# Expert weights in 32 KB runs: halves of 4 MB in the loop, smaller pieces and a new order of work for the last two experts

## The chip, the cores and the metric

One core of a Trainium2 chip. The metric is device time in microseconds (us) of one launch, lower is better; a time is the median of several runs.

## What is computed

One decoder layer for 256 prompt tokens with 16 meta tokens ahead of them, and 8 sample tokens: two mixers, then a mixture of 32 experts with 4 of them for each token, then a last norm. All weights are fp32, and nearly all the bytes are the experts': `w_gu` is 32 x 1024 x 2048 (8 MB an expert), `w_down` 32 x 1024 x 1024 (4 MB an expert), 403 MB of the 431 MB read.

```python
x = x + (g_a * branch_a + g_b * branch_b) @ w_o
logits = (xt @ w_router) + b_router                  # xt = rms_norm(x, g_ffn)
gates = softmax(top_k(logits, 4))
# for each expert e, over the tokens that chose it:
hgu = xblk @ w_gu[e] + b_gu[e]
gate = minimum(hgu[:, :1024], 7.0)
up = clip(hgu[:, 1024:], -7.0, 7.0)
act = gate * sigmoid(1.702 * gate) * (up + 1)
y = act @ w_down[e] + b_down[e]                      # times the gate, added to x by token
y_prompt, y_sample = rms_norm(x, g_final)            # meta tokens dropped
```

## The kernel before

**Front, up to about 175 us.** The input projection, both mixers and `w_o` run in split precision. Then, tile by tile (two of 128 tokens, one of the 8 samples), the new rows `Y` are normed, turned and routed. For the gather, a row of `Y` times its norm is kept as three bf16 parts in `XP`: ScalarE's `part` (L732) rounds the first, VectorE's `keep_rest` (L1477) subtracts it, `next_part` and `keep_third` make the other two. The first expert has a shorter way (L1101).

**An expert is an item i** (64 token slots; `more` further rounds exist for fuller experts and are not run here). TensorE does, in this order: `gate_up(i)`, eight rows k of `gu_ring`, each 4 products of 128 x 512 (shown as x8); the scatter of expert i-2 after rows 2, 4 and 6 (one token tile each, high and low parts into banks 6 and 7); `way_back(i-1)`, which turns `pick_twice` into the matrix that sends slots back to tokens; `gather` for i+1; `down(i-1)`, eight rows of `down_ring`; `turn(i)`, which transposes gate and up. Around it ScalarE copies the gate half (`keep_gate`), takes the sigmoid, copies the way back (`back`) and rounds the expert's result to `y_high` (`high`); VectorE does the SwiGLU (`swiglu`), adds scattered rows to `Y` (`add_rows`, L1628), makes `pick_twice` (`make_twice`, L1592 to L1596) and `pick`, copies the up half and makes `y_low` (`low_part`).

**Loads.** All of the experts' weights come by SyncE (SP), one queue, in program order. `gu_ring` has 16 slots of one row (8 KB a partition), eight for even and eight for odd experts; `down_ring` has eight slots of 4 KB. `load_gu` (L419 to L423) brings two rows in one load of 2 MB: partition p takes matrix rows 2p and 2p+1 of a block of 256, so a run is 16 KB. `load_row` brings one row, 1 MB in runs of 8 KB. `load_down` brings four rows, 2 MB in runs of 16 KB. Each load waits until TensorE has used what lay in its slots: `gu_used` counts rows of gate-up, `down_used` pairs of rows of down. The order is gate-up of i+2, then down of i, with the second half of a gate-up put behind the down for experts 9 to 19 (`HALVED`). The last expert's down weights go to slots 0 to 3 of `gu_ring` in four loads of 1 MB (L542), once gate-up of expert 30 is done.

**Deal of the rows.** Since row k of a gate-up block holds matrix rows of one residue, every operand of that product follows it: the transposes of `Y` (`by_row`), the gather's slices of `XP`, `wr`, `g_ffn`.

**The end.** For the last two: `gate_up(31)`, `way_back(30)`, `turn(31)`, `down(30)`, `way_back(31, 5)`, then `down(31)` with the scatters of 30 after its rows 1, 3 and 5 into banks 6, 0 and 2 (`LAST_BANKS`), then the scatters of 31, the additions, the norm (L593, L1717, L1719) and the stores.

## Time and profile before

| | |
|---|---|
| median of 3 runs | 1090.71 us (1090.71 to 1091.31) |
| the profiled execution | 1091.32 us, its span 1089.5 us |
| TensorE (PE) busy | 1049.2 us, 96% |
| VectorE, ScalarE busy | 462.5 us, 174.2 us |
| read from HBM | 431.10 MB, 397 GB/s over the span |

A busy PE is a PE with matmuls in it, also while they are fed slowly. How much of the span each stage takes and what it waits for must be read from the slices, the chain of work and the timeline. In a timeline row the bracket names how long the engine was idle before and what ended that; PEld are the weight loads of TensorE, SPq is SyncE's queue, in which only the issue of a load shows, not its transfer.

### The profile page before, as it was taken

Reading aid. Unit: us, or ns where it says so; the run is one execution under the profiler, and the core shown is the slowest. Engines: PE = TensorE matmul, PEld = TensorE weight load, DVE = VectorE, ACT = ScalarE, POOL = GpSimd, SP = SyncE. Lnnn points to the kernel's source line nnn. Section 1 sums busy time; section 2 is a strip of 40 time slices with the busy share of each in tenths; the row PEclk is TensorE's granted clock in tenths of the full one; section 3 lists DMA queues with packets and bytes.
Section 4 is the critical chain, followed back from the end, with each engine's and each line's share of the span. In section 5 each row is a group of like instructions: output and inputs, shape, how many; then the busy total and the mean of one; then the engine's idle time right before and its main releaser. Section 6 shows DMA issues by size and latency. Waiting matters only on the chain.

```text
span 1089.5 us, 17315 instructions
## 1 busy us (share of the span) xinstructions
PE 1049.2 (96%) x7081; PEld 510.2 (47%) x7081; DVE 462.5 (42%) x780; ACT 174.2 (16%) x296; POOL 8.9 (1%) x21
## 2 busy tenths in 40 slices
PE   8999999999999999999999999999999999999995
PEld 7999975434433444434344333333444333333332
DVE  5577675333333333333333333333333333333344
ACT  5435533100000000000000000000000000000012
POOL 1000100000000000000000000000000000000000
PEclk9999999999999999999999999999999999999998
DMA  9872899999999999999999999999999999999994
GB/s 295 289 227 103 324 405 375 429 420 426 428 429 427 429 428 430 427 429 428 429 428 428 429 428 428 428 429 428 428 429 428 429 428 429 429 428 431 426 425 170
DMA packets 52479, 432.63 MB, mean 397 GB/s; under 512 B 4630, under 2 KB 21546, under 8 KB 26205
## 3 DMA queue, kind: packets, MB, share of 16 engines
q1 hardware_dynamic: 50959, 431.04, 95.3%
q10 hardware_dynamic: 1494, 1.22, 0.4%
q8 instruction: 19, 0.31, 0.1%
q14 instruction: 7, 0.06, 0.0%
HBM read 431.10 MB, written 1.39 MB: 397 GB/s over the span
## 4 chain that ended last, share of the span: by engine, by line
PE 65%; DMA 26%; DVE 4%; issue 4%; ACT 1%; SPq 1%; DVEq 0%; ACTq 0%
PE PS L1153 24%; PE PS L1182 17%; DMA down_ring<-in_w_down_dram 14%; DMA gu_ring<-in_w_gu_dram 11%; PE PS L918 9%; PE PS L1082 3%; PE PS L1122 2%; PE PS L949 2%; PE PS L1124 1%; PE PS L1196 1%; PE PS L1166 1%; PE PS L1164 1%; DVE pick_twice L1596 1%; PE PS L1200 1%; PE PS L869 0%
## 5 line engine op out<-in xcount | busy, mean ns | idle before, releaser
L1153 PE MATMUL PS<-gu_ring,XgT 128*64 128x512 f32 x2048 | 470.5, 599 | 6.7 <-DMA gu_ring<-in_w_gu_dram 6.7
L1153 PEld LDWEIGHTS PS<-gu_ring,XgT 128*64 128x64 f32 x2048 | 134.5, 136 | 272.0 <-issue 244.5
L1182 PE MATMUL PS<-down_ring,actT 128*64 128x512 f32 x984 | 219.3, 596 | 7.7 <-DMA down_ring<-in_w_down_dram 7.7
L1628 DVE TENSOR_TENSOR Y<-PS,Y 128x1024 f32<-128x1024 f32 (+1 forms) x96 | 117.0, 1220 | 253.7 <-PE PS L1124 253.7
L1182 PEld LDWEIGHTS PS<-down_ring,actT 128*64 128x64 f32 x984 | 67.5, 137 | 134.8 <-issue 119.3
L1666 DVE SCALAR_TENSOR_TENSOR y_low<-PS,slot_gate,y_high 128x512 fp32r<-128x512 f32 x31 | 23.3, 750 | 228.6 <-ACT y_high L804 228.6
L816 ACT ACTIVATE work<-PS 128x512 f32<-128x512 f32 x32 | 19.1, 597 | 454.8 <-PE PS L1153 454.8
L918 PE MATMUL PS<-h_high,win_high 128*128 128x264 f32 (+2 forms) x256 | 71.2, 287 | 0.0
L918 PE MATMUL PS<-h_high,win_low 128*128 128x264 f32 (+2 forms) x256 | 70.9, 286 | 0.0
L918 PE MATMUL PS<-h_low,win_high 128*128 128x264 f32 (+2 forms) x256 | 70.8, 285 | 0.0
L804 ACT ACTIVATE y_high<-PS,slot_gate 128x512 fp32r<-128x512 f32 x31 | 21.3, 687 | 258.9 <-PE PS L1182 258.9
L1082 PE MATMUL PS<-pick,XP 128*128 128x64 bf16 x1768 | 56.7, 193 | 0.0
L1082 PEld LDWEIGHTS PS<-pick,XP 128*128 128x128 bf16 x1768 | 56.1, 99 | 0.8 <-issue 0.8
L1122 PEld LDWEIGHTS PS<-y_high,spread 64*128 64x128 f32 x186 | 17.3, 183 | 75.5 <-issue 74.6
L918 PEld LDWEIGHTS PS<-h_high,win_high 128*128 128x128 f32 x256 | 47.4, 189 | 0.4 <-issue 0.2
L1317 DVE TENSOR_TENSOR win_low<-gu_ring,win_high 128x2048 fp32r<-128x2048 f32 x15 | 34.4, 2293 | 30.7 <-ACT win_high L619 30.6
L918 PEld LDWEIGHTS PS<-h_low,win_high 128*128 128x128 f32 x256 | 47.4, 188 | 0.0
L918 PEld LDWEIGHTS PS<-h_high,win_low 128*128 128x128 f32 x256 | 47.3, 188 | 0.0
L1122 PE MATMUL PS<-y_high,spread 64*128 64x512 f32 x186 | 46.6, 498 | 0.0
L1643 DVE TENSOR_TENSOR work<-PS,bias_gu 128x512 f32<-128x512 f32 x64 | 44.0, 687 | 1.2 <-PE PS L1200 0.6
L1564 DVE TENSOR_TENSOR XgT<-PS,params 128x512 f32<-128x512 f32 x31 | 21.4, 691 | 53.5 <-PE PS L1082 53.5
L1124 PE MATMUL PS<-y_low,spread 64*128 64x512 f32 x186 | 36.6, 391 | 0.0
(236 smaller groups left out, 778.2 us busy)
## 6 DMA issues: line engine op xcount, KB each, us to landing
gu_ring<-in_w_gu_dram SPq DMA_DIRECT2D x119, 2048.0 KB, 28.5
down_ring<-in_w_down_dram SPq DMA_DIRECT2D x60, 2048.0 KB, 21.2
gu_ring<-in_w_gu_dram SPq DMA_DIRECT2D x18, 1024.0 KB, 10.0
gu_ring<-in_w_in_dram SPq DMA_DIRECT2D x16, 1024.0 KB, 9.4
gu_ring<-in_w_down_dram SPq DMA_DIRECT2D x4, 1024.0 KB, 28.3
down_ring<-in_w_down_dram SPq DMA_DIRECT2D x3, 1024.0 KB, 9.4
down_ring<-in_w_pool_up_dram SPq DMA_DIRECT2D x1, 2048.0 KB, 11.6
gu_ring<-in_w_conv_out_dram SPq DMA_DIRECT2D x2, 1024.0 KB, 6.2
```

Of the source, the lines that this page charges most:

```text
L918: return mm(PS[:, n % 4, 0:COLS - lo], w[:, k, P * (n % 2):P * (n % 2) + P], h[:, k, lo:COLS], start=first, stop=final)
L949: last = mm(PS[:, 4 + n % 4, 0:TOK], of(w, k, m), x[:, k, :], start=(k == 0 and part == 0), stop=(k == CH - 1 and part == 2))
L1082: last = mm(rows if rows is not None else PS[:, 5, SLOTS * k:SLOTS * k + SLOTS], XP[:, part, 2 * P * m:2 * P * m + 2 * P].rearrange("t (p ...
L1122: mm(PS[:, bank + h, :], way[rows, t, :], y_high[rows, :], start=True, stop=False)
L1124: last = mm(PS[:, bank + h, :], way[rows, t, :], y_low[rows, :], start=False, stop=True)
L1153: last = mm(PS[SLOTS * h:SLOTS * h + SLOTS, b, :], XgT[:, k, :], w[:, D * b + HALF * h:D * b + HALF * h + HALF], start=(k == 0), stop=(k = ...
L1182: last = mm(PS[SLOTS * h:SLOTS * h + SLOTS, bank, :], acts[:, f % 4, f // 4, :], rows[:, f, HALF * h:HALF * h + HALF], start=(f == 0), sto ...
L1317: tt(win_low[:, b % WIN_SLOTS, :], gu_ring[:, b % WIN_SLOTS, :], win_high[:, b % 2, :].bitcast(F32), ALU.subtract).then_inc(win_ready, 1)
L1564: tt(XgT[:], PS[:, 5, :].rearrange("p (k s) -> p k s", k=KT), g_ffn_cols.unsqueeze(2).to_broadcast([P, KT, SLOTS]), ALU.mult).then_inc(xg_ ...
L1628: tt(Y[rows, t, :].rearrange("p (h n) -> p h n", h=2), PS[rows, bank:bank + 2, :], Y[rows, t, :].rearrange("p (h n) -> p h n", h=2), ALU.a ...
L1643: tt(hgu[:, HALF * b:HALF * b + HALF].rearrange("p (c s) -> p c s", s=SLOTS), PS[:, 2 + b, :].rearrange("p (c s) -> p c s", s=SLOTS), bias ...
L1666: stt(y_low[:], PS[:, bank, :], gate[:], y_high[:].bitcast(F32), ALU.mult, ALU.subtract).then_inc(low_ready, 1)
```

## The change

Gate-up weights come in loads of 4 MB (`load_half`): partition p takes four matrix rows of a block of 512, a run of 32 KB. One semaphore for each half (`half_landed`) takes the place of one for each two rows, and TensorE waits at rows 0 and 4. The loads of expert 2 and the first half of expert 3 stay in smaller pieces, with semaphores of their own. The deal of rows goes from two to four everywhere: `by_row`, `wr`, `g_ffn`; `part` and `keep_rest` now read `Y` in steps of four elements (`dealt`) and write `XP` in row order, so that the gather reads it without a step. Three single bf16 products (`fill_early`) are added in the front.

At the end, expert 30 comes in 2 MB pieces, expert 31's rows 0 to 3 in two of 2 MB and 4 to 7 in four of 1 MB, the down weights of 30 in four of 1 MB, those of 31 in three of 1 MB and two of 512 KB. Both last ways back move into the last gate-up, behind rows 3 and 5, with `spread_last` now for expert 30 and `spread` for 31; `turn(31)` moves behind two rows of `down(30)`. The last scatters are split: all high parts first, then the low parts. On VectorE `make_twice` moves ahead of the row additions, in every item. The diff, cut to what the text speaks of (the rest are `wr`, `g_ffn`, the new semaphores, and calls that follow):

```diff
--- before.py
+++ after.py
...
@@ -218,6 +218,12 @@
         pool_up = down_ring[:, CH:2 * CH, :]
         pool_high = by_rows(win_low[:, 4:6, :])
         conv_out, conv_low, conv_high = gu_ring[:, 0:2, :], win_low[:, 0:2, :], win_low[:, 2:4, :]
+
+        def dealt(cols):
+            return cols.rearrange("t (p r) -> t r p", r=CH)
+
+        def by_fours(cols):
+            return cols.rearrange("t (r p) -> t r p", r=CH)
...
@@ -412,16 +425,23 @@
...
-            def load_row(e, parity, k):
-                m, r = divmod(k, 2)
+            def load_row(e, parity, k, signal=None):
+                h, r = divmod(k, CH)
                 sp.dma_start(gu_ring[:, KT * parity + k, :],
-                             w_gu[0, e, 2 * P * m:2 * P * m + 2 * P, :].rearrange("(p r) n -> p r n", r=2)[:, r, :]
-                             ).then_inc(gu_landed[CH * parity + m], 16)
-
-            def load_gu(e, parity, m):
-                src = w_gu[0, bass.ds(e, 1), 2 * P * m:2 * P * m + 2 * P, :].rearrange("a (p r) n -> (a p) (r n)", r=2)
+                             w_gu[0, e, HALF * h:HALF * h + HALF, :].rearrange("(p r) n -> p r n", r=CH)[:, r, :]
+                             ).then_inc(signal or gu_landed[CH * parity + k // 2], 16)
+
+            def load_gu(e, parity, m, signal):
+                h, q = divmod(m, 2)
+                src = w_gu[0, bass.ds(e, 1), HALF * h:HALF * h + HALF, :].rearrange("a (p q r) n -> (a p) q (r n)", q=2, r=2)
                 sp.dma_start(gu_ring[:, KT * parity + 2 * m:KT * parity + 2 * m + 2, :].rearrange("p s n -> p (s n)"),
-                             src).then_inc(gu_landed[CH * parity + m], 16)
+                             src[:, q, :]).then_inc(signal, 16)
+
+            def load_half(e, parity, h):
+                src = w_gu[0, bass.ds(e, 1), HALF * h:HALF * h + HALF, :].rearrange("a (p r) n -> (a p) (r n)", r=CH)
+                at = KT * parity + CH * h
+                sp.dma_start(gu_ring[:, at:at + CH, :].rearrange("p s n -> p (s n)"), src
+                             ).then_inc(half_landed[2 * parity + h], 16)
...
@@ -467,17 +487,24 @@
...
-            def item_gu(i, e, parity, chunks=range(CH)):
-                for m in chunks:
-                    sp.wait_ge(gu_used, 8 * i + (2 * m - 14))
-                    load_gu(e, parity, m)
+            def item_gu(i, e, parity, halves=range(2)):
+                for h in halves:
+                    sp.wait_ge(gu_used, 8 * i + (4 * h - 12))
+                    load_half(e, parity, h)
+
+            def item_chunk(i, e, parity, m, signal):
+                sp.wait_ge(gu_used, 8 * i + (2 * m - 14))
+                load_gu(e, parity, m, signal)
 
 
             for k in range(2):
                 sp.wait_ge(gu_used, k + 1)
-                load_row(2, 0, k)
-            item_gu(2, 2, 0, (1, 2, 3))
-            item_gu(3, 3, 1)
+                load_row(2, 0, k, third_rows)
+            for m, signal in ((1, half_landed[0]), (2, third_chunk), (3, half_landed[1])):
+                item_chunk(2, 2, 0, m, signal)
+            for m, signal in ((0, fourth_chunk), (1, half_landed[2])):
+                item_chunk(3, 3, 1, m, signal)
+            item_gu(3, 3, 1, (1,))
...
@@ -493,7 +520,7 @@
...
-            first, second = (0, 1), (2, 3)
+            first, second = (0,), (1,)
...
@@ -512,7 +539,7 @@
...
-            with sp.Fori(0, E // 2 - 2 - AHEAD - HALVED) as pair:
+            with sp.Fori(0, E // 2 - 3 - AHEAD - HALVED) as pair:
...
@@ -527,22 +554,37 @@
...
+            before, last = more * E + (E - 2), more * E + (E - 1)
+            for m in range(CH):
+                item_chunk(before, E - 2, 0, m, gu_landed[m])
+            item_down(more * E + (E - 3), E - 3)
+            for m in range(2):
+                item_chunk(last, E - 1, 1, m, gu_landed[CH + m])
+            for k in range(CH, KT):
+                sp.wait_ge(gu_used, 8 * last + (k - 15))
+                load_row(E - 1, 1, k, last_rows[k - CH])
+
+            def down_rows(e, first, n):
+                h, j = divmod(first, CH)
+                return w_down[0, e, HALF * h:HALF * h + HALF, :].rearrange("(p j) n -> p j n", j=CH)[:, j:j + n, :]
+
+            for q in range(CH):
+                sp.wait_ge(down_used, 4 * before + (q - 3))
+                sp.dma_start(down_ring[:, 2 * q:2 * q + 2, :], down_rows(E - 2, 2 * q, 2)).then_inc(before_landed[q], 16)
             sp.wait_ge(gu_used, more * (8 * E) + 8 * (E - 1))
-            for q in range(CH):
-                h, j = q // 2, 2 * (q % 2)
-                sp.dma_start(down_last[:, 2 * q:2 * q + 2, :],
-                             w_down[0, E - 1, HALF * h:HALF * h + HALF, :].rearrange("(p j) n -> p j n", j=CH
-                                                                                     )[:, j:j + 2, :]
-                             ).then_inc(last_landed[q], 16)
+            for q in range(CH - 1):
+                sp.dma_start(down_last[:, 2 * q:2 * q + 2, :], down_rows(E - 1, 2 * q, 2)).then_inc(last_landed[q], 16)
+            sp.dma_start(down_last[:, 6:7, :], down_rows(E - 1, 6, 1)).then_inc(last_landed[3], 16)
+            sp.dma_start(down_last[:, 7:8, :], down_rows(E - 1, 7, 1)).then_inc(last_row_landed, 16)
...
@@ -729,7 +771,7 @@
...
-                nc.scalar.activation(dst, Y[rows, t, cols], ACT.Copy, scale=stat[rows, 3, t:t + 1]
+                nc.scalar.activation(by_fours(dst), dealt(Y[rows, t, cols]), ACT.Copy, scale=stat[rows, 3, t:t + 1]
                                      ).then_inc(first_part, 1)
...
@@ -844,13 +886,18 @@
...
             last, before = more * E + (E - 1), more * E + (E - 2)
-            keep_gate(last, False, before)
+            sigmoid(before)
+            back(before, spread_last, slot_gate_last)
+            act.wait_ge(scattered, more * (3 * E) + 3 * (E - 2))
+            back(last, spread, slot_gate, 5)
+            act.wait_ge(gu_used, more * (8 * E) + 8 * E)
+            act.wait_ge(act_ready, before + 1)
+            nc.scalar.activation(hgu[:, 0:HALF], PS[:, 0, :], ACT.Copy).then_inc(gate_kept, 1)
             sigmoid(last)
             nc.scalar.preload_act_table(ACT.Sqrt)
-            back(last, spread_last, slot_gate_last, 5)
-            high(before)
+            high(before, slot_gate_last)
             act.wait_ge(scattered, more * (3 * E) + 3 * (E - 1))
-            high(last, slot_gate_last, 5)
+            high(last, slot_gate, 5)
...
@@ -1020,6 +1067,10 @@
...
+
+            def fill_early():
+                mm(PS[:, 1, :].rearrange("p (c n) -> p c n", c=CH), ones[:], ones[:].unsqueeze(1).to_broadcast([P, CH, P]),
+                   start=True, stop=True)
...
@@ -1067,9 +1118,11 @@
...
             pe.wait_ge(pick_early, 1)
+            fill_early()
             pe.wait_ge(resid, 5)
             turn_rows(1, 1)
             turn_tails()
+            fill_early()
             pe.wait_ge(x2_kept, 5)
...
@@ -1088,6 +1140,7 @@
...
+            fill_early()
             pe.wait_ge(mask_ready, 3)
             count(1, ones[:], 2, True, False)
...
@@ -1116,12 +1169,19 @@
...
-            def scatter(t, way=spread, bank=6):
+            def scatter_part(t, way, part, first):
+
+                for h in range(2):
+                    rows = slice(SLOTS * h, SLOTS * h + SLOTS)
+                    last = mm(PS[:, LAST_BANKS[t] + h, :], way[rows, t, :], part[rows, :], start=first, stop=not first)
+                return last
+
...
@@ -1137,16 +1197,23 @@
...
                 for k in range(KT):
                     if by_halves and k == CH:
                         pe.wait_ge(xg_ready, 1)
-                    if k % 2 == 0:
-                        by_row = 16 if k == 0 and u == 0 and two_before is not None else 0
-                        pe.wait_ge(gu_landed[CH * u + k // 2], landed + by_row)
+                    if between and k >= CH:
+                        pe.wait_ge(last_rows[k - CH], 16)
+                    elif chunks and k % 2 == 0:
+                        pe.wait_ge(gu_landed[CH * u + k // 2], landed)
+                    elif not chunks and k % CH == 0:
+                        if k == 0:
+                            pe.wait_ge(*((fourth_chunk, 16) if u else (third_rows, 32)))
...
@@ -1156,6 +1223,8 @@
...
                     if two_before is not None and k in (2, 4, 6):
                         scatter_item(two_before, k // 2 - 1)
+                    if between and k in between:
+                        way_back(*between[k])
...
 
...
-                item(2 * pair + 2, 0, 16 * pair + 48, 2 * pair + 1, 2 * pair)
-                item(2 * pair + 3, 1, 16 * pair + 48, 2 * pair + 2, 2 * pair + 1)
+                item(2 * pair + 2, 0, 16 * pair + 16, 2 * pair + 1, 2 * pair)
+                item(2 * pair + 3, 1, 16 * pair + 16, 2 * pair + 2, 2 * pair + 1)
...
 
             last, before, two_before = from_end(1), from_end(2), from_end(3)
-            landed = more * (8 * E) + (8 * E + 16)
-            item(before, 0, landed, two_before, from_end(4))
-
-            gate_up(last, 1, landed, two_before)
-            way_back(before)
-            turn(last)
-            down(before)
-            way_back(last, 5)
-            pe.wait_ge(added, more * (3 * E) + (3 * (E - 3) + 4))
-            down(last, down_last, last_landed, 5, before, act_last)
+            item(before, 0, 48, two_before, from_end(4), chunks=True)
+
+            gate_up(last, 1, 48, two_before, chunks=True, between={3: (before,), 5: (last, 5)})
+            pe.wait_ge(spread_ready, 2 * last + 2)
+            pe.wait_ge(act_ready, before + 1)
+            for f in range(KT):
+                if f == 2:
+                    turn(last)
+                if f % 2 == 0:
+                    pe.wait_ge(before_landed[f // 2], 16)
+                down_row(f, down_ring, actT[:], 4)
+            pe.wait_ge(act_ready, last + 1)
+            for f in range(KT):
+                if f % 2 == 0:
+                    pe.wait_ge(last_landed[f // 2], 16)
+                elif f == KT - 1:
+                    pe.wait_ge(last_row_landed, 16)
+                down_row(f, down_last, act_last, 5)
+                if f in (1, 3, 5):
+                    t = f // 2
+                    if t == 0:
+                        pe.wait_ge(low_ready, before + 1)
+                        pe.wait_ge(added, more * (3 * E) + (3 * (E - 3) + 4))
+                    scatter_part(t, spread_last, y_high, True)
+                    scatter_part(t, spread_last, y_low, False).then_inc(scattered, 1)
+            pe.wait_ge(high_ready, last + 1)
+            for t in range(NT):
+                pe.wait_ge(added, more * (3 * E) + (3 * (E - 2) + t + 2))
+                scatter_part(t, spread, y_high, True)
             pe.wait_ge(low_ready, last + 1)
             for t in range(NT):
-                pe.wait_ge(added, more * (3 * E) + (3 * (E - 2) + t + 2))
-                scatter(t, spread_last, LAST_BANKS[t])
...
@@ -1474,8 +1557,8 @@
...
                 v.wait_ge(first_part, n + 1)
-                stt(rests[(t, h)][rows, :], Y[rows, t, cols], stat[rows, 3, t:t + 1], src, ALU.mult, ALU.subtract
-                    ).then_inc(first_rest, 1)
+                stt(by_fours(rests[(t, h)][rows, :]), dealt(Y[rows, t, cols]), stat[rows, 3, t:t + 1], by_fours(src),
+                    ALU.mult, ALU.subtract).then_inc(first_rest, 1)
...
@@ -1676,11 +1759,10 @@
             def item(i, after, before=None, e_before=0, two_before=None, biases=False):
                 if before is not None:
                     swiglu(before, e_before)
+                    make_twice(before)
                 if two_before is not None:
                     for t in range(NT):
                         add_rows(two_before, t)
-                if before is not None:
...
@@ -1699,14 +1781,19 @@
...
             last, before, two_before = more * E + (E - 1), more * E + (E - 2), more * E + (E - 3)
-            item(last, None, before, E - 2, two_before)
+            swiglu(before, E - 2)
+            make_twice(before)
+            add_rows(two_before, 0)
             v.wait_ge(spread_turned, before + 1)
             make_twice(last)
+            for t in range(1, NT):
+                add_rows(two_before, t)
+            keep_up(last, before)
             swiglu(last, E - 1, act_last)
-            low_part(before)
+            low_part(before, slot_gate_last)
             for t in range(NT):
                 add_rows(before, t, LAST_BANKS[t])
-            low_part(last, slot_gate_last, 5)
+            low_part(last, slot_gate, 5)
```

## Rows read from the trace of the kernel before

**Rows 1.** The page's forty slices of the span (27.2 us each), DMA and GB/s.
```profile
DMA  9872899999999999999999999999999999999994
GB/s 295 289 227 103 324 405 375 429 420 426 428 429 427 429 428 430 427 429 428 429 428 428 429 428 428 428 429 428 428 429 428 429 428 429 429 428 431 426 425 170
```

**Rows 2.** Chain of work, 237 to 270 us: start, length, what.
```profile
239.15 7.02 PE PS L1182 x32
246.17 0.68 PE PS L1196 x4
247.33 5.30 PE PS L1153 x24
...
257.54 3.58 PE PS L1153 x16
...
262.03 0.94 issue
...
263.97 0.55 PE PS L1164 x3
...
265.08 1.66 PE PS L1082 x56
266.73 3.58 PE PS L1182 x15
```

**Rows 3.** Chain of work, 600 to 700 us.
```profile
605.54 25.48 DMA down_ring<-in_w_down_dram
```

**Rows 4.** DMA view, 500 to 900 us: queue, packets, MB, share of 16 engines.
```profile
q1 hardware_dynamic: 11771, 171.37, 100.6%
```

**Rows 5.** DMA view, 1062 to 1067 us, within the last down loads (8 KB runs).
```profile
q1 hardware_dynamic: 289, 2.11, 101.2%
```

**Rows 6.** Timeline, 985 to 1090 us, PE: start, length, engine, line, operation, idle before.
```profile
993.24 1.94 PE L1153 MATMUL PS<-gu_ring,XgT 128*64 128x512 f32 x8 [0.42 <-DMA gu_ring<-in_w_gu_dram]
...
1038.27 3.65 PE L1153 MATMUL PS<-gu_ring,XgT 128*64 128x512 f32 x16
...
1042.21 1.94 PE L1153 MATMUL PS<-gu_ring,XgT 128*64 128x512 f32 x8 [0.29 <-DMA gu_ring<-in_w_gu_dram]
...
1051.98 1.94 PE L1153 MATMUL PS<-gu_ring,XgT 128*64 128x512 f32 x8 [0.43 <-DMA gu_ring<-in_w_gu_dram]
...
1058.86 7.09 PE L1182 MATMUL PS<-down_ring,actT 128*64 128x512 f32 x32
...
1067.63 1.94 PE L1182 MATMUL PS<-gu_ring,work 128*64 128x512 f32 x8 [0.64 <-ACT slot_gate_last L799]
```

**Rows 7.** The same timeline behind the last down product, three engines.
```profile
1077.29 0.69 ACT L804 ACTIVATE y_high<-PS,slot_gate_last 128x512 fp32r<-128x512 f32 x1 [9.13 <-PE PS L1182]
1078.01 0.75 DVE L1666 SCALAR_TENSOR_TENSOR y_low<-PS,slot_gate_last,y_high 128x512 fp32r<-128x512 f32 x1 [1.46 <-ACT y_high L804]
...
1078.89 0.50 PE L1122 MATMUL PS<-y_high,spread_last 64*128 64x512 f32 x2 [1.73 <-DVE y_low L1666]
...
1079.23 0.39 PE L1124 MATMUL PS<-y_low,spread_last 64*128 64x512 f32 x2
...
1079.66 3.47 DVE L1628 TENSOR_TENSOR Y<-PS,Y 128x1024 f32<-128x1024 f32 x3 [0.90 <-PE PS L1124]
```

**Rows 8.** Timeline of SP's queue, 226 to 243 us: issues of loads.
```profile
227.60 8.83 SPq L423 DMA_DIRECT2D gu_ring<-in_w_gu_dram  x3
```

**Rows 9.** By tile: the one down_ring load issued at 218.6 us.
```profile
DMA to landing us min/median/max: 10.8/10.8/10.8
```

**Rows 10.** By tile: the one gu_ring load (1 MB) issued at 176.7 us.
```profile
DMA to landing us min/median/max: 5.1/5.1/5.1
```

**Rows 11.** Groups by line and form, VectorE: busy, mean ns of one, idle.
```profile
L1477 DVE SCALAR_TENSOR_TENSOR rest_high<-Y,stat,XP 128x512 f32<-128x512 f32 x1 | 0.7, 747 | 0.0
...
L1291 DVE COPY bias_gu<-PS 128x256 f32<-128x256 f32 x2 | 1.1, 604 | 0.0
```

**Rows 12.** Timeline, 172 to 176 us, PE: the fills of before.
```profile
172.18 0.59 PE L1026 MATMUL PS<-XP,ones 128*128 128x512 bf16 x2
```

## Prediction of the change's time

> **What bounds the kernel now.** I read the page's forty slices first: from the sixth of them to the last but one the sixteen DMA engines are 90% busy or more, at 420 to 431 GB/s in all but the first two [rows 1]. Then the chain of work in order of time. It has two regimes. In the first half of the loop it runs through TensorE alone: from one down product to the next is 266.73 - 239.15 = 27.58 us for one expert [rows 2]. In the second half it is a load of down_ring, 25.48 us of the chain, with a little of TensorE in between, again and again [rows 3]. An expert is six loads of 2 MB. The DMA view of 500 to 900 us has 171.37 MB in 400 us, 428.4 GB/s, so 4.895 us for 2 MB and 29.37 us for six [rows 4]: the second regime is the loads' own time. The first isn't a gain in hand: loads moved at the same rate then [rows 1] and TensorE only used up what lay ready. So the loads set the time at which any late piece of weights is there, and what follows the last such wait is TensorE's.
>
> Where is that last wait? In the timeline of the last three experts TensorE waits for a load at 993.24 (rows 6, 7 of expert 29), at 1042.21 and at 1051.98 (rows 2 and 6 of expert 31) [rows 6]. After 1051.98 it doesn't wait for a load again: its down product of 30 begins at 1058.86, of 31 at 1067.63, and the last copy out at 1077.29 [rows 6, 7].
>
> **Part 1, 4 MB halves.** Bytes, order and buffers stay. A load of 2 MB in runs of 16 KB becomes part of one of 4 MB in runs of 32 KB. Before's trace has no such load, so its price is a line through the two that it has: 16 KB runs, 4.895 us for 2 MB [rows 4]; 8 KB runs (the last down loads), 2.11 MB in 5 us, 2.485 us for 1 MB [rows 5]; each is eight runs an engine and one signal. Twice the 8 KB load less one 16 KB load is 4.970 - 4.895 = 0.075 us of fixed time per eight runs. A 4 MB load, by the line, takes 2 x 4.895 - 0.075 = 9.715 us. Halves: one of expert 3, two each of experts 4 to 29, 53 in all, so **53 x 0.075 = 4.0 us earlier**. Bounds: the 8 KB row is 257 runs, uncertain by some 1%, which makes 0.075 anything from 0.02 to 0.13: 1 to 7 us; and nothing at all if the lost time isn't per run (a rival). I take the row's own value.
>
> **Part 2, coarser waits in the loop.** For SP: the slots of a half come free after its fourth row, not its second, and SP is in order, so the down loads behind it wait too. TensorE gains 2 us an expert on the loads, and by as much the queue deepens, so the thin place is the first one. It is expert 4. In before the load ahead of it, issued at 218.6, lands 10.8 us later, at 229.4 [rows 9]. Now the first half of expert 4 needs four rows of expert 2, and those are done at 227.60, when before issues its second 2 MB [rows 8]. A load issued into an empty queue at 176.7 took 5.1 us to land, 1 MB, 2.485 of it data [rows 10]: so 2.6 us of latency. The half lands at 227.6 + 2.6 + 9.7 = 239.9 against 229.4 + 9.7 = 239.1 behind a full queue: **0.8 us later**, and all that follows with it. Bounds: 0 (the engines don't finish together, and the latest has the least gap) and 2.6. Expert 4's second half is free near 236, needs 2.6 and its turn comes at 239.9: covered; from there on the lead grows by 29.2 - 27.2 = 2 us an expert.
>
> For TensorE: it starts rows 4 to 7 when 4 MB have landed. In the loads' regime its 27.58 us stand against 29.2, so it is there first and only waits. What it costs shows at the end, part 4.
>
> **Part 3, the dealt order.** Rows of a matrix go to the partitions in fours instead of pairs, so ScalarE's first parts and VectorE's rests read Y in steps of 16 bytes. A rest takes 747 ns [rows 11] and a first part about as long; two small-tile ones and two of ScalarE's, later two of VectorE's, stand on the way to expert 0's first row. TensorE already reads in steps of 16 bytes: four transposes of work take 0.68 us, three of the contiguous pick_twice 0.55, 0.17 and 0.18 each [rows 2]. Against it: VectorE's copy into bias_gu in steps of 64 bytes took 604 ns for 256 elements [rows 11], 2.36 ns each against 1.46. If all six paid that, it is 6 x 512 x 0.9 ns = 2.8 us. First what the row shows, then the rule: the Trainium skill, "SBUF — State Buffer", Door 1, says that SBUF has lines of 16 bytes and wants two accesses in each for full rate; by it a step of four fp32 pays and the step of two didn't. The transposes, on another engine, say otherwise. I take **0.2 us**, between 0 and 2.8, nearest to the transposes, since those read, as here, and the copy writes. The three fill_early products stand ahead of waits; a pair of fills takes 0.59 us [rows 12], so one at most 0.3: 0 while the wait behind it is as long, 0.9 in all if none is; I take 0. Gathers lose a stride, the router and g_ffn only their order: 0.
>
> **Part 4, the end.** Now expert 29's rows 4 to 7 wait for one landing, at L, which is where before has 993.24. Experts 30 and 31 come in 2 MB, 1 MB and 0.5 MB pieces, so I follow TensorE from L. make_twice goes ahead of the row additions: the "issue" of 0.94 us that waits for it [rows 2] shows as 0.35 us of TensorE per expert, gone: 27.58 - 0.35 = 27.23. Row 4 begins 7.75 us into gate-up (5.30 for three rows, a scatter of 0.66, a row of 1.8), and the whole of it takes 16.3: row 7 follows the scatter that begins at 257.54 + 3.58 = 261.12, at 261.8, and takes 1.8 [rows 2]. From L:
> to gate-up 30: 27.23 - 7.75 = 19.5;
> to gate-up 31: 27.2, 46.7;
> its eight rows with three scatters 16.3, and both ways back inside, 1.1 each: 65.2;
> down of 30 and turn 31: 7.0 + 1.2, 73.4;
> down of 31 with scatters, 1077.20 - 1067.63 = 9.6: **83.0**.
> Before: 1077.20 - 993.24 = **84.0**. So 1.0 us less. What it replaces: before waited some 2 us in all (for rows 2, 4 and 6 of expert 31, ahead of the way back, and for the spread at 1067) but began gate-up 31 at 1038.27, 45.0 after L; now it begins 1.7 later, because expert 29 is not done until four rows after L. Is a load late? After L come ten of 4.895, then eleven of 2.485 and two halves of that, 78.8 us, and TensorE asks for the last row at 82.1: 3.3 us of cover. The DVE and ACT waits: twice of 31 needs the way back of 30 turned (about 1 us of VectorE, against 5 us until row 5's end); ScalarE's second back needs the third scatter of 29, two rows before the spread is asked for. Both covered. Bounds 3 less (if the late start is caught up) and 2 more (a way back that stalls between rows: its 1.1 us twice).
>
> High parts of the last scatter first: y_high is done at 1077.98, TensorE starts at 1078.89 after y_low, first addition at 1079.66 [rows 7]. Three high pairs, 0.34 us each by the step from the first pair to the next, nearly fit into the 0.75 us of y_low; the first low pair then is done 0.3 us sooner than four products were. **0.3 us less**, 0 to 0.5.
>
> **Sum.** -4.0 + 0.8 + 0.2 - 1.0 - 0.3 = -4.3 us. The profiled execution took 1091.32 us, 1.8 beside its span of 1089.5; it is the slowest of three whose median is 1090.71. All terms are differences, so I take them from the median: 1090.7 - 4.3 = **1086.4 us**.
>
> **Rivals.**
> A. The 1.6% of a load that isn't at the pace of a longer one isn't per run. Then the halves bring nothing and -0.3 is left: 1090.4. For it: a row of 5 us carries the whole slope. Against: in that row the engines are as busy as in the other (101.2% and 100.6%) and move less [rows 4, 5].
> B. Slower. The 128 runs of a load begin 32 KB apart in HBM, where all of before's expert loads have 16 KB. If that spacing costs, every half pays. Price by a row: at the pace of the 8 KB loads a half takes 4 x 2.485 = 9.94 us, 0.15 over 9.79 for two loads, 53 x 0.15 = 8.0 us slower in place of 4.0 faster: -0.3 + 8.0, 1098.4. It decides from 0.006 us a half, the point at which -0.3 is used up. No row has another spacing for such a load, so nothing speaks for it but that it is untried. [...]
> C. The strided reads cost what the bias_gu copy does: +2.8 in place of 0.2, 1089.0; all of it passes to the end, since expert 0's rows free the slots for expert 2.
> D. The end is late: the ways back stall the last gate-up or the gap at 228 us is the full 2.6, +3: 1089.4.
>
> **How the numbers follow.** Forecast 0.55, its own range 1083.5 to 1088.5; A 0.17; B 0.10; C 0.09; D 0.09. A measurement of this kernel tells about 0.2%, 2.2 us, from no change, so faster is under 1088.5. Faster: the forecast and a little of C and D, which start above it, 0.61. Slower: B, and a sum of C and D with A, 0.12. The same: 0.27. The range for 8 in 10 leaves out B and the best of the forecast: 1083.0 to 1091.5.
>
> **What would show it.** Steps: the chain of late experts at 29.2 us in place of 29.36 (halves land 9.7 apart); DMA busy without a hole around 228 us, or with one; expert 0's first row at 174.8; L about 3 us before 993.24; 83.0 us from there to y_high; no load waited for in the last down product. Wrong if halves land 9.79 or more apart, if expert 0 starts a microsecond late, or if TensorE has waits inside the last gate-up.

## The result, and the profile after

The changed kernel takes **1094.52 us** (median of 7 runs, 1094.37 to 1096.6) against 1091.04 for the kernel before beside it (1090.71 to 1092.03): ratio 1.0037, 95% interval 1.0026 to 1.0049. It is slower by 3.5 us where I forecast 4.3 faster, and lies outside the range. The profiled execution took 1096.6 us with a span of 1094.8; before's was 1091.32, so the two traces are 5.28 us apart, and the working below is about these. It is the slowest of the seven, 2.1 us above their median, and has their lowest mean clock (0.991, where the others have 0.992 to 0.996).

The page's slices of after first (they answer [rows 1]; before's clock row had a 9 in each slice but the last, an 8):

```profile
PEclk9999997999999999999999999999999999999999
DMA  9872896999999999999999999999999999999994
GB/s 300 282 230 97 334 399 265 437 369 425 434 427 433 424 430 431 435 431 429 427 431 431 430 432 433 432 429 426 432 436 425 436 426 436 426 436 423 427 420 198
```

Taken together, the slices from the tenth on move more than before's. But slice 7 has 265 GB/s for before's 375, slice 9 has 369 for 420, and in slice 7 TensorE's granted clock is not full. Both losses lie before 250 us. TensorE's timeline of after around slice 7 (start, length, engine, line, operation, tiles, count, and in brackets the idle time before it and what ended it):

```profile
165.46 1.97 PE L1057 MATMUL PS<-wr,work 128*128 128x32 f32 x16 [0.93 <-ACT work L788]
167.27 1.68 PE L1032 MATMUL PS<-wo_low,m_high 128*128 128x512 f32 x4
...
177.59 3.74 PE L1154 MATMUL PS<-before_spread,Y 128*128 128x64 f32 x16
181.27 15.65 PE L1220 MATMUL PS<-gu_ring,XgT 128*64 128x512 f32 x64
```

TensorE waits 0.93 us for ScalarE, then works slowly (the four products of L1032 took 1.17 us in before), and expert 0's first row comes at 181.27. In before it came at 174.74:

```profile
174.74 13.96 PE L1153 MATMUL PS<-gu_ring,XgT 128*64 128x512 f32 x64
```

The clock by stretches of after (the columns: stretch, its length, then busy time and count of PE, PEld, DVE, ACT and POOL, the granted clock, DMA share, GB/s):

```profile
165.00:168.00 3.00, 2.54 (x19) 2.39 (x20) 1.82 (x5) 2.71 (x5) 0.00 (x0) 0.95 0.98 396
168.00:172.00 4.00, 4.00 (x20) 3.57 (x19) 3.18 (x11) 0.86 (x3) 0.00 (x0) 0.50 1.03 434
172.00:176.00 4.00, 4.00 (x42) 3.75 (x41) 1.20 (x8) 2.93 (x4) 0.00 (x0) 0.50 0.99 418
176.00:180.00 4.00, 3.78 (x26) 3.30 (x25) 3.04 (x6) 1.06 (x2) 0.00 (x0) 0.76 0.18 72
180.00:184.00 4.00, 4.00 (x14) 2.11 (x16) 2.46 (x9) 1.77 (x3) 0.00 (x0) 0.67 0.00 0
...
220.00:230.00 10.00, 10.00 (x50) 3.83 (x48) 3.43 (x5) 1.26 (x2) 0.00 (x0) 1.00 0.99 387
230.00:240.00 10.00, 10.00 (x50) 3.27 (x48) 5.07 (x8) 0.06 (x1) 0.00 (x0) 1.00 0.77 297
240.00:250.00 10.00, 10.00 (x103) 4.82 (x101) 3.03 (x5) 1.15 (x3) 0.00 (x0) 1.00 1.04 441
```

The last three stretches in before:

```profile
220.00:230.00 10.00, 10.00 (x50) 3.21 (x48) 4.78 (x9) 0.63 (x1) 0.00 (x0) 1.00 1.01 408
230.00:240.00 10.00, 9.68 (x99) 4.71 (x101) 4.96 (x9) 1.15 (x3) 0.00 (x0) 1.00 1.01 427
240.00:250.00 10.00, 10.00 (x52) 3.93 (x50) 2.82 (x5) 1.32 (x2) 0.00 (x0) 1.00 1.01 426
```

Right behind the wait the granted clock is 0.50, that is 1.2 GHz, for eight microseconds, and it is not full again until 188 (0.90 from 184 on). From 180 to 184 no byte moves: expert 2's loads need slots that expert 0 has not freed. The second hole, 230 to 240, is the one that I looked for at 228. An idle stretch alone does not bring the clock down: in the loop TensorE waits 1.88 us up to 970.50, and the granted clock stays at 1.00 there and behind it.

**The books of the profiled run.** A way to read a hole is to count what the loads are short of. From 160 to 220 us after's stretches add up to 2.8 MB less than before's, 6.6 us at 428 GB/s. From 220 to 250 (387, 297 and 441 GB/s against 408, 427 and 426) another 1.36 MB, 3.2 us. That is 9.8 us behind at 250. TensorE's waits for a load in experts 28 and 29 of after, and in expert 28 of before:

```profile
970.50 1.94 PE L1220 MATMUL PS<-gu_ring,XgT 128*64 128x512 f32 x8 [1.88 <-DMA gu_ring<-in_w_gu_dram]
...
999.64 1.94 PE L1220 MATMUL PS<-gu_ring,XgT 128*64 128x512 f32 x8 [1.71 <-DMA gu_ring<-in_w_gu_dram]
```

```profile
963.88 1.94 PE L1153 MATMUL PS<-gu_ring,XgT 128*64 128x512 f32 x8 [0.44 <-DMA gu_ring<-in_w_gu_dram]
```

L, the landing for which row 4 of expert 29 waits, is 999.64, 6.4 us after 993.24 [rows 6]: 9.8 less 3.4 that the halves brought by then. The 3.4 is what is left over; a count of its own, the DMA views of 250 to 960 us, has 305.70 MB in after and 304.16 in before, 3.6 us. The first addition of the last scatter, which was at 1079.66 [rows 7]:

```profile
1082.86 0.69 ACT L846 ACTIVATE y_high<-PS,slot_gate 128x512 fp32r<-128x512 f32 x1 [8.71 <-PE PS L1251]
```

```profile
1083.67 0.96 PE L1176 MATMUL PS<-y_high,spread 64*128 64x512 f32 x6 [0.94 <-ACT y_high L846]
```

```profile
1084.92 3.47 DVE L1711 TENSOR_TENSOR Y<-PS,Y 128x1024 f32<-128x1024 f32 x3 [0.59 <-PE PS L1176]
```

5.26 us later than before, with 5.28 in the whole time. So the end gave 1.1 us back, the halves 3.4, and what happens before 250 us took 9.8. That is what the experiments are about.

### The profile page after: what moved, and what is told of

Its sections match the earlier page's. It is cut to its first block, busy times and chain, and to the rows that moved or that the text cites. A ratio compares the mean times of both kernels' runs of the same rounds, so it can differ in the third digit from the quotient of the medians.

```text
span 1094.8 us, 17121 instructions
## 1 busy us (share of the span) xinstructions
PE 1053.5 (96%) x7085; PEld 517.0 (47%) x7086; DVE 467.7 (43%) x780; ACT 177.1 (16%) x296; POOL 8.9 (1%) x21
## 4 chain that ended last, share of the span: by engine, by line
PE 61%; DMA 35%; DVE 2%; issue 1%; ACT 1%; SPq 0%; ACTq 0%; DVEq 0%
PE PS L1220 22%; DMA down_ring<-in_w_down_dram 21%; PE PS L1251 15%; DMA gu_ring<-in_w_gu_dram 14%; PE PS L965 9%; PE PS L1134 3%; PE PS L996 2%; PE PS L1182 2%; PE PS L1184 1%; PE PS L1235 1%; PE PS L1261 1%; PE PS L1233 1%; PE PS L1265 1%; PE PS L1057 0%; PE PS L916 0%
```

## The experiments

Each run stands with its median beside before's on the same chip in the same set (1091.0 to 1091.4), the ratio and its interval. For most runs the interval is about 1 us to either side, so a difference between two runs of less than that is not clear of noise.

**Natural order** (XP as before; the gathers step over it):

```diff
-nc.scalar.activation(by_fours(dst), dealt(Y[rows, t, cols]), ACT.Copy, ...)
+nc.scalar.activation(dst, Y[rows, t, cols], ACT.Copy, ...)
-stt(by_fours(rests[(t, h)][rows, :]), dealt(Y[rows, t, cols]), ..., by_fours(src), ...)
+stt(rests[(t, h)][rows, :], Y[rows, t, cols], ..., src, ...)
-XP[:, part, P * k:P * k + P],
+XP[:, part, HALF * m:HALF * m + HALF].rearrange("t (p r) -> t r p", r=CH)[:, q, :],
```

> The changed kernel with ScalarE's first parts and VectorE's rests written in the natural order of the columns again (contiguous reads), and the gathers reading XP in steps of four columns; halves, fills and the new end stay. Theory 1 (the 8.2 us that gate-up 1 starts late come from the reads in steps of 16 bytes, through ScalarE, a TensorE wait of 0.93 us and the granted clock that is then 0.50 for some 10 us): a first part of ScalarE takes 1.34 for two again, the granted clock is 1.00 from 160 to 190 us, expert 0's first row comes at 174.5 to 175, and the time is 1094.5 - 8.2 = 1086.3 us (1085 to 1088). Rival 1 (fill_early, the new landing order or the clock by itself make the front late): it starts after 179 us and the time stays over 1092.

1092.4 us, ratio 1.001 (1.0001 to 1.0019): 2.1 us better than after, not 8.2, so neither theory holds as it stood. ScalarE's and VectorE's operations by form, 155 to 190 us, after's and then this kernel's (count | busy us, mean ns of one | idle before):

```profile
L774 ACT ACTIVATE XP<-Y,stat 128x512 bf16<-128x512 f32 x4 | 4.7, 1210 | 1.1 <-DVE stat L1551 1.1
...
L1560 DVE SCALAR_TENSOR_TENSOR rest_high<-Y,stat,XP 128x512 f32<-128x512 f32 x1 | 1.1, 1134 | 0.0
```

```profile
L774 ACT ACTIVATE XP<-Y,stat 128x512 bf16<-128x512 f32 x4 | 2.7, 715 | 0.6 <-DVE stat L1552 0.6
...
L1561 DVE SCALAR_TENSOR_TENSOR rest_high<-Y,stat,XP 128x512 f32<-128x512 f32 x1 | 0.7, 743 | 0.0
```

The wait and the low clock behind it are gone, yet expert 0 starts at 176.53, 1.8 late:

```profile
176.53 13.95 PE L1221 MATMUL PS<-gu_ring,XgT 128*64 128x512 f32 x64
```

The reason is something I had at nothing: the sixteen products of expert 0's last gather read Y itself, as weights, now in steps of 16 bytes (8 in before). Before's weight loads, then this kernel's (duration in ns, least/median/most):

```profile
L1101 PEld LDWEIGHTS PS<-before_spread,Y x16: 193/196/197, 172.7 to 174.5; 128*128 128x128 f32 x16
```

```profile
L1155 PEld LDWEIGHTS PS<-before_spread,Y x16: 308/329/332, 172.7 to 176.1; 128*128 128x128 f32 x16
```

3.95 us in place of 2.10 at a granted clock of 1.00, and 3.74 in after at a lower one: at 16 bytes the load sets the pace, not the clock. This kernel's runs have mean clocks from 0.994 to 0.997, and their times follow (0.997: 1090.6 to 1091.4; 0.994: 1093.9 to 1094.0); before's lie between 0.996 and 0.998. This order has a price of its own: the gathers of the loop now read XP in steps of 8 bytes, and the 56 products of one take 2.03 us in place of 1.79 (at 1003.63 and, in after, at 1009.25).

**Fills ahead of the wait** (four `fill_early()` before `pe.wait_ge(x2_kept, 4)` in after):

> The changed kernel with its strided reads, and four fill products more (some 0.29 us each) ahead of the wait for the kept transposes at 164.5 us, where TensorE stood idle for 0.93 us. If the clock falls only for that idle stretch, the granted clock stays at 1.00 through 165 to 190, expert 0 starts at 181.3 less some 4 to 5 us (the work at half clock), and the time is 1089 to 1091: what is left over the natural order is the strided reads' own price, some 2 to 3 us. If the clock falls for another reason (the fills change nothing of it), 1094 to 1095.

1094.06 us, 1.0022 (1.0013 to 1.0032). The idle stretch is filled (1.04 us of products at 164.92) and the clock stays at 1.00 until 176; then, behind the slow gather, it falls to 0.64 from 180 to 184. Expert 0 starts at 178.97:

```profile
178.97 4.05 PE L1222 MATMUL PS<-gu_ring,XgT 128*64 128x512 f32 x10
```

So the wait does cause the first fall, but the time is the 1094 to 1095 that I expected if the fills did nothing: keeping the first fall off leaves most of the loss, and a second fall follows the slow weight loads.

**Halves as two loads in runs of 16 KB** (natural order kept):

```diff
+for m in (2 * h, 2 * h + 1):
+    load_gu(e, parity, m, half_landed[2 * parity + h])
-sp.dma_start(gu_ring[:, at:at + CH, :].rearrange("p s n -> p (s n)"), src).then_inc(half_landed[2 * parity + h], 16)
```

> The first kernel of this set with every half from expert 4 on issued as two loads of 2 MB in runs of 16 KB, with the same waits and the same one point at which TensorE may start four rows. Only the length of a run in HBM differs. My price of 0.075 us of fixed time per eight runs an engine: 52 halves x 0.075 = 3.9 us slower than the first kernel, and landings of the late experts' 4 MB 9.79 apart. Rival A (nothing is fixed per run; the halves gain nothing): the same within 0.5 us. Rival (TensorE's coarser wait, not the run, is what the halves change): also the same, since the wait is kept.

1096.61 us, 1.005 (1.0036 to 1.0064): 4.2 us slower than natural order, with the same waits. The mean clocks of the five runs lie somewhat lower (0.994 to 0.996); between runs of equal clock the difference is 3.5 to 4.1 us. The DMA view of 500 to 900 us, which answers [rows 4]; after, then this kernel:

```profile
q1 hardware_dynamic: 7941, 172.33, 100.5%
```

```profile
q1 hardware_dynamic: 11759, 171.38, 100.6%
```

171.38 MB is before's 171.37. After's is 0.56% more in the same time, 4.2 us over the 750 us of the loop (natural order has 172.26 MB). Rival A is out. So is B: this kernel's runs of 16 KB begin 32 KB apart where before's begin 16 KB apart, and the rate is the same. Two things differ between the two kernels, the length of a run and the number of loads; which of them holds the fixed time, no run tells apart.

**Steps of 8 bytes** (the kernel before with parts and rests dealt in pairs):

> The kernel before with one part of the change alone, at half the stride: first parts and rests read Y in steps of 8 bytes (columns dealt in pairs), the gathers read XP contiguous. If only steps of 16 bytes cost (the rule of 16-byte lines), a ScalarE first part takes 0.67 us and a rest 0.75 us as before, and the time is 1091.0. If every step over one element costs, they take 1.18 and 1.13 us as in the changed kernel, the clock falls as there, and the time is 1097 to 1099.

```profile
L738 ACT ACTIVATE XP<-Y,stat 128x512 bf16<-128x512 f32 x4 | 2.8, 752 | 0.6 <-DVE stat L1474 0.6
...
L1483 DVE SCALAR_TENSOR_TENSOR rest_low<-Y,stat,XP 128x512 f32<-128x512 f32 x1 | 0.7, 748 | 0.0
```

1091.15 us, 1.0001 (0.9992 to 1.001), as in the first theory. Steps of 8 bytes are nearly free (752 and 748 ns), steps of 16 are not (1210 and 1134).

**Expert 0 in pairs** (natural order; expert 0's weight rows, its g_ffn columns and its gathers in pairs):

```diff
-last = mm(first_rows(k), by_row(P, 1, k), pick_first, ...)
+last = mm(first_rows(k), by_row(P, 1, k, 2), pick_first, ...)
```

> The natural-order kernel (first run of the first set) with expert 0 alone put back to the deal in pairs: its weight rows, its g_ffn columns, and the sixteen products of its last gather, whose weights TensorE then reads from Y in steps of 8 bytes in place of 16. Theory: those loads cost 0.24 us each at 16 bytes and 0.12 at 8, also where the granted clock is 1.00, 1.85 us in all, and in some runs the slack engine lets the clock fall behind them. So the last gather takes 2.1 us again, expert 0's first row comes at 174.6 to 174.9, the mean clock is 0.997 in every run, and the time falls by 1.9 to 3 us, to 1089.5 to 1090.5. Rival (the gather's length is hidden, since the loads of the loop don't follow TensorE's start): the time stays at 1092.

1090.0 us, 0.9988 (0.9979 to 0.9997); clock 0.997 or 0.998 in all eleven runs. Its weight loads, and its stretches around the second hole:

```profile
L1163 PEld LDWEIGHTS PS<-before_spread,Y x16: 193/196/197, 173.0 to 174.8; 128*128 128x128 f32 x16
```

```profile
220.00:230.00 10.00, 10.00 (x51) 3.32 (x49) 6.23 (x11) 0.72 (x2) 0.00 (x0) 1.00 0.86 314
230.00:240.00 10.00, 10.00 (x101) 5.19 (x101) 3.78 (x6) 1.15 (x3) 0.00 (x0) 1.00 0.94 403
240.00:250.00 10.00, 10.00 (x50) 3.83 (x48) 2.74 (x5) 1.05 (x2) 0.00 (x0) 1.00 0.97 413
```

Expert 0 starts at 175.04:

```profile
175.04 13.95 PE L1229 MATMUL PS<-gu_ring,XgT 128*64 128x512 f32 x64
```

The front is whole, and the second hole is still there, 1.31 MB or 3.1 us. Against after, this much undoing of the deal is worth 4.5 us by the medians. But with it gone the kernel is 1.4 us faster than before, not the 4.5 that the other terms of my sum add up to.

**The hole.** Expert 4's first half as two loads (e6); expert 3's second half and all of expert 4 (e9), here the core of e9:

```diff
-item_gu(3, 3, 1, (1,))
+item_chunk(3, 3, 1, 2, fourth_third)
+item_chunk(3, 3, 1, 3, half_landed[3])
-item_gu(4, 4, 0)
+for m, signal in ((0, fifth_chunk), (1, half_landed[0]), (2, fifth_third), (3, half_landed[1])):
+    item_chunk(4, 4, 0, m, signal)
```

> The kernel with expert 0 in pairs, and expert 4's first half as two loads of 2 MB again, each issued when its two slots are free and each waited for by itself; experts 2 to 5 stand outside TensorE's loop for that. Theory 2 (the hole in the DMA engines' work at 225 to 242 us comes from the wait of that one half for four rows of expert 2, with a latency of 2.6 us on an empty queue): the bytes landed by 250 us rise by what 1.5 to 2.5 us of the full rate bring, and the time falls by as much, to 1087.5 to 1088.5. Rival (the hole comes from expert 3's second half and the down loads behind it): the hole only shrinks by under 0.5 us and the time stays.

1090.9 us, 0.9992 (0.9983 to 1.0001), where 1087.5 to 1088.5 was expected: 1.9 us of bytes are missing in place of 3.1 (375, 385 and 419 GB/s), the time is not better. In e7, whose early loads are the same, 2.8 us are missing (367, 380 and 395), so even the 1.2 us got back are not sure. The wait for row 7 of expert 2, ahead of the second half (issued at 237.44), took over, as e9 bears out. I had called that half covered.

> The kernel with expert 0 in pairs, with expert 3's second half and both halves of expert 4 as loads of 2 MB, each issued as soon as its two slots are free and each waited for by itself (three of 53 halves undone). The kernel with expert 4's first half alone in chunks had 2.0 us of the full rate's bytes missing between 220 and 245 us where the one with the half had 3.3, and the slowest engine landed that half at the same time. Theory (the hole is made of three waits, of which the second, for row 7 of expert 2, takes over when the first is gone): now the bytes landed by 250 us stand within 0.5 us of the kernel before's, and the time is 1090.0 less 2 to 3 us, 1087 to 1088. Rival (what sets the loads' time afterwards is the slowest of the 16 engines, and it doesn't lie in the hole): the bytes are there, but the time stays within 0.7 us of 1090.0.

1089.4 us, 0.9984 (0.9975 to 0.9993). This is 0.6 less than with halves, within the noise, and not the 2 to 3 expected: the bytes are back, and the time is the rival's, within 0.7 us of 1090.0. Its stretches:

```profile
230.00:240.00 10.00, 10.00 (x100) 4.93 (x97) 3.56 (x5) 1.15 (x3) 0.00 (x0) 1.00 1.01 428
240.00:250.00 10.00, 10.00 (x54) 3.97 (x53) 2.50 (x5) 0.69 (x1) 0.00 (x0) 1.00 1.00 424
250.00:275.00 25.00, 25.00 (x170) 10.02 (x167) 8.76 (x15) 2.02 (x5) 0.00 (x0) 1.00 0.99 415
```

Full rate until 250 (0.5 us short in all), and then 415 GB/s over 25 us where before has 428, 0.8 us: the hole has moved on, to where expert 5's first half is issued.

**Expert 29 in four loads** (e7 on e6, e10 on e9).

> The kernel of the run before it, and expert 29 in four loads of 2 MB, each waited for by itself, in place of two halves. Theory 3 (TensorE's wait for a whole half costs at the end only): its idle 1.5 to 1.7 us ahead of row 4 of expert 29, from where it runs to the end without a wait, falls to 0.4 or moves to a later load, and the time falls by 1.2 to 1.6 us, two more fixed times of 0.075 included. Rival (the loads of experts 30 and 31 have no cover left and take the place of that wait): TensorE waits again in expert 30 or 31, and less than 0.5 us is gained.

> The run before it, with expert 29 in four loads of 2 MB too. In the earlier pair of kernels that took 1.5 us from the stretch between the wait in expert 28 and the last additions, and 0.6 us from the median. Expected: 0.6 to 1.5 us faster than the run before it. Rival (once the loads lead, those of experts 30 and 31 have no cover): the same.

1090.28 us for e7, 0.9989 (0.998 to 0.9998), and **1088.51** for e10, 0.9978 (0.9969 to 0.9987). The wait ahead of expert 29's row 4 is gone in both, and none for a load comes in expert 30 or 31; e7's last one is this, in expert 28:

```profile
964.57 1.94 PE L1242 MATMUL PS<-gu_ring,XgT 128*64 128x512 f32 x8 [1.64 <-DMA gu_ring<-in_w_gu_dram]
```

From the wait in expert 28 to the first addition it is 113.4 us in e7 (to 1077.93) and 114.9 in e6 (964.02 to 1078.89). Of this 1.5 the medians show 0.6 (less than the 1.2 to 1.6 expected of e7) and 0.9 (within what was expected of e10); either alone is within the noise.

**Expert 5 too** (on e10):

> The best kernel so far (expert 0 in pairs; expert 3's second half, expert 4 and expert 29 in loads of 2 MB) with expert 5 in loads of 2 MB as well. In the run before, the missing bytes moved from 225-245 us to 250-275 us, 1.0 us of the full rate, where expert 5's halves are issued. Theory (the hole walks on to the next half, and gets smaller with each expert, since the loads take 29.2 us an expert and TensorE 27.4): nothing over 0.3 us is missing at 250 to 275 us now, the bytes landed by 300 us are within 0.5 us of the kernel before's, and the time is 0.4 to 1.0 us lower, 1087.5 to 1088.1. Rival (what is missing there comes from the slowest engine's drift, not from a wait): the same bytes at 300 us and the same time.

1088.19 us, 0.9973 (0.9963 to 0.9983). The stretch from 250 to 275 us is at 427 GB/s, before's has 428, so the hole there was a wait. The gain of 0.3 us, less than expected, is within the spread of the runs. TensorE waits for a load in experts 30 and 31 again (0.35 us at 1021.94, 0.41 at 1041.51). This is the fastest kernel of the study, and against 1090.0 its 1.8 us (1.5 by the ratios) are more than one interval's half width: the small loads of experts 3, 4, 5 and 29 help together, though no step among them is clear by itself.

**No fills**, and the deal **on the writing side**:

> The kernel with expert 0 in pairs, without the three single fill products of the front. My price for them was 0. Expected: expert 0's first row at 174.7 to 175.0 as with them, granted clock 1.00 through the front, the same time within 0.7 us of 1090.0. Rival (they hold the clock up): a granted clock under 1.00 between 165 and 190 us and 1 to 3 us more.

1089.35 us, 0.9982 (0.9973 to 0.9992), clock 1.00 through the front. Against 1090.0 with the fills: they bring nothing here, and what they may cost, 0.6 us, lies within the spread of the runs.

> The changed kernel with the deal moved from the reading to the writing side: ScalarE reads Y contiguous and writes XP in steps of 256 bytes, VectorE's rests stay contiguous and its third parts are read and written in such steps; gathers stay contiguous. If only fp32 reads in steps of 16 bytes cost, a first part of ScalarE takes 0.67 us and the front is that of the natural order, 1091 to 1093. If strided writes cost as reads do, they take 1.1 us or more, the clock falls at 165 us, and the time is 1094 to 1097.

1105.83 us (two runs, ratio 1.0134, 1.0115 to 1.0152), far outside both theories: a first part of ScalarE takes 2.69 us.

```profile
L780 ACT ACTIVATE XP<-Y,stat 128x512 bf16<-128x512 f32 x4 | 9.8, 2692 | 3.2 <-DVE stat L1557 3.2
...
L1576 DVE TENSOR_TENSOR XP<-XgT,XP 128x512 bf16<-128x512 f32 x1 | 2.7, 2660 | 0.0
```

TensorE stands idle from 165 to 168 us, the clock is 0.50 from 168 to 184, and expert 0 starts at 191.34.

## Why the prediction was wrong

**Part 3 is the step that failed.** I priced it at 0.2 us of 0 to 2.8. It cost 6.5 at the start of expert 0 (174.74 to 181.27) in the profiled execution, and 4.5 in the median time (1094.52 to 1090.0 when it is undone; 4.9 with each set against its own before). The runs take the 6.5 apart by that start, one profiled execution each:

| kernel | expert 0's first row | what it adds |
|---|---|---|
| before | 174.74 | |
| expert 0 in pairs | 175.04 | 0.3, less than one run differs from another (174.69 in e10, 175.58 in e6, with the same front) |
| natural order | 176.53 | 1.5: the last gather's loads at 16 bytes |
| fills ahead of the wait | 178.97 | 2.4: ScalarE's and VectorE's reads at 16 bytes |
| after | 181.27 | 2.3: the granted clock |

In the run with fills TensorE is 0.54 us late already ahead of them (the products of L1032 begin at 164.00, in after at 163.46), so the last two terms are nearer 1.9 and 2.8. The gate-up of expert 0 adds 1.7 (15.65 against 13.96), and as much with the fills, behind the second fall. That expert 0 starts more than a microsecond late is the sign of being wrong that I had named. Three errors, in order of what they teach. First, the row: I went by TensorE's transposes, which take 0.14 us each either way, and not by the copy into bias_gu, because "those read, as here". The transposes were another engine; their loads of Y take 208 ns at 8 bytes and at 16, where the gather's go from 196 to 329, and no run shows why. The copy's 0.9 ns an element was nearly right: a ScalarE part grew by 0.50 us for 512 elements, 0.97 ns each, a VectorE rest by 0.39, 0.76 each. Rival C held the truth of it at 0.09. First the rows, then the rule: the loads of 196 and 329 ns, parts of 752 and 1210 and rests of 748 and 1134 at 8 and 16 bytes. The rule of lines of 16 bytes with two accesses in each (the Trainium skill, "SBUF — State Buffer", Door 1), which I set aside, has the break between these two steps. The trace agrees in the parts, the rests and the gather's loads, not in the transposes.

Second, an operation was left off the list. "Gathers lose a stride" is true of those that read XP; the one that reads Y went from 8 to 16 bytes. Its products took 1.85 us more (3.95 against 2.10).

Third, a delay on the way of TensorE was counted once, as its own length. An idle stretch of 0.93 us was followed by a granted clock of 0.50, and that cost 2.3 us more by the start of expert 0. Neither my bounds nor a rival had the clock in them. That the wait brings the first fall is shown by the fills; the size of its cost is the difference of two executions.

**Part 2, the thin place.** Place and mechanism were right, the size in bytes was not: 0.8 us forecast, 3.1 missing with a whole front, 3.2 in after. One reason is how I counted. I took the landing by the slowest engine and found it nearly met. But an engine that is done early may stand idle until the next load comes, and before had that load in the queue; the DMA share of 0.77 from 230 to 240 us fits this, and no view shows it by engine. The other is that I followed one wait. Expert 4's second half wasn't covered (e6), and with both in chunks the third wait showed, at expert 5 (e9, e12). How much of the missing bytes ends up in the time is open. For: in the kernel with expert 0 in pairs L is 992.54, 0.7 us early, which is 3.1 behind at 250 less the 3.8 that its bytes from 250 to 960 us (305.81 MB) are ahead. Against: e6 got up to 1.2 us back and gained nothing, e9 got 2.6 back at 250 us and 1.8 of them net of its next hole, and gained at most 0.6. From 250 to 960 us e9 moves only 305.09 MB, 1.7 us less; a part of the gain is lost again there, and no run shows by what.

**Part 1** was right: 4.0 forecast; 4.2 by the pair of kernels that differ in the loads alone (3.5 to 4.1 at equal clock), 3.6 by the bytes from 250 to 960 us, 3.4 in the profiled run's books by L. Late waits are 29.14 us apart (970.50 to 999.64), 29.2 forecast.

**Part 4** was right: from L to y_high 83.2 us against 84.05 in before (993.24 to 1077.29, [rows 6, 7]), 1.0 less forecast and 0.8 measured; from y_high to the first addition 2.06 against 2.37, 0.3 less as forecast. In the kernels with natural order it is 83.7 to y_high: two of their longer gathers lie on the way. No load is waited for in the last gate-ups, and the ways back stall nothing. L itself was forecast 3 us early and came 6.4 late, which is Parts 2 and 3. With Part 3 undone it comes 0.7 early, and of the 3.1 us by which that kernel misses the other terms' 4.5, Part 2's bytes make 2.3 and the two longer gathers 0.5; the rest is within the noise. An expert in TensorE's regime takes 27.2 us, as worked out:

```profile
246.98 7.02 PE PS L1251 x32
...
274.19 7.02 PE PS L1251 x32
```

**The fills** cost nothing that can be told, as assumed. TensorE's coarser wait for expert 29 was in the 83.0, but not priced by itself: undoing it gives 1.5 us from expert 28 to the end in the traces, 0.6 and 0.9 in the medians.

## What to carry over

A layout change is paid at each reader of the data, so list them all, and price each by a row of the same engine in the same role with the new step; where no row has it, let the nearest other engine's price stand as the likely value and not as the far bound. On a serial path such as this front, look at what the granted clock does behind a new idle stretch as well; in the loop longer ones cost nothing of it. When loads are merged, go through every wait in front of them in turn: taking away the worst shows the next, and the first experts, before the queue has a lead, can keep the small loads. Count what that brings in time and not only in bytes: here the bytes came back and most of the time did not.

## What was new about the hardware

- fp32 reads of 512 elements a partition: contiguous, in steps of 8 and of 16 bytes 715, 752 and 1210 ns on ScalarE, 743, 748 and 1134 on VectorE. TensorE's weight load of 128 x 128 fp32 ahead of a product: 196 ns at 8 bytes, 329 at 16; ahead of a transpose 208 at either. Of 128 x 128 bf16: 98 ns contiguous, 118 in steps of 8 bytes.
- The same ScalarE copy with its bf16 output in steps of 256 bytes: 2692 ns. VectorE's subtraction with such a step on one input and the output: 2660, against 684; its rest with such a step on the bf16 input alone: 1155, against 743.
- An idle stretch of TensorE of 0.93 us in the front was followed by eight microseconds at 1.2 GHz, and by none when it was filled. Sixteen slow weight loads were followed by a fall too in some executions (0.64 from 180 to 184 us with the fills, 0.50 from 176 to 180 with the halves as two loads) and in another not (natural order, 1.00 throughout). In the loop an idle stretch of 1.88 us was followed by none.
- Loads of 4 MB in runs of 32 KB move 0.5% more than loads of 2 MB in runs of 16 KB (172.33 and 171.38 MB in 400 us); runs of 16 KB that begin 32 KB apart move as much as those that begin 16 KB apart (171.38 and 171.37).
